# Building part of the expert gates by scatter-add instead of one-hot matmuls, and moving gathered rows between two passes

## The reference

```
q = x @ w_q                                   # 8 heads, two halves of 64
s = q . keys                                  # 2 x 128 scores per head
top_s, top_i = top_k(s, 16)                   # on each half
best_s, best_j = top_k(top_s[0] + top_s[1], 16)
expert = i1 * 128 + i2                        # 8 heads x 16 experts per token
g = softmax(best_s)
act = gelu(u[expert] . x) * g                 # u, v: tables of 16384 x 1024
y = sum over the 128 choices of act * v[expert]
```

## Time and profile before

| | us |
|---|---|
| median of 3 runs (lowest, highest) | 2739.08 (2737.34, 2743.43) |
| the profiled execution, its span | 2744.57, 2742.8 |
| PE busy | 2465.3 (90%) |
| DVE busy | 2131.3 (78%) |
| ACT busy | 1234.8 (45%) |
| POOL busy | 571.3 (21%) |

### The profile page before, as it was taken

One profiled execution on the slowest core, in us unless ns is written; L12 is line 12 of the kernel. 1 busy time (PEld: TensorE's weight loads), 2 busy tenths in 40 slices (PEclk: granted clock), 3 DMA queues, 4 the chain that ended last, 5 costly groups with the idle time before them and its releaser, 6 DMA issues.

```text
span 2742.8 us, 36197 instructions
## 1 busy us (share of the span) xinstructions
PE 2465.3 (90%) x10956; PEld 1938.4 (71%) x10956; DVE 2131.3 (78%) x3891; ACT 1234.8 (45%) x2704; POOL 571.3 (21%) x408
## 2 busy tenths in 40 slices
PE   4987888999899787899999999998878999999996
PEld 3767766666456576777777777776756888878885
DVE  4877613666388855889999999989688888888888
ACT  2332043444312142267777787777433333333333
POOL 2013104422032320011111111112122323232221
PEclk9999999999999899999999999999988999999998
DMA  6646651112032325478888888888899999999996
GB/s 275 217 163 253 255 218 62 62 62 86 23 117 101 146 78 217 136 263 309 322 299 319 298 319 309 305 304 313 318 387 347 381 382 388 384 368 380 389 382 237
DMA packets 223810, 697.60 MB, mean 254 GB/s; under 512 B 15840, under 2 KB 111456, under 8 KB 181472
## 3 DMA queue, kind: packets, MB, share of 16 engines
q1 hardware_dynamic: 165984, 367.25, 37.2%
q0 software_dynamic: 37632, 270.55, 26.0%
q10 hardware_dynamic: 20096, 58.72, 5.6%
HBM read 614.67 MB, written 81.79 MB: 254 GB/s over the span
## 4 chain that ended last, share of the span: by engine, by line
PE 42%; DVE 32%; DVEq 9%; DMA 8%; issue 5%; ACT 3%; SPq 1%; ACTq 1%; POOL 0%; PEldq 0%; PEld 0%
PE ps L866 21%; PE ps L557 7%; DVE g_acc L1787 5%; DVEq L1799 4%; PE ps L542 4%; DVE rows L1778 4%; DVE arena L1454 3%; DMA act_in<-act_scratch 3%; DVE hot L1741 2%; PE ps L569 2%; DMA arena<-in_weights 2%; DVE cand L1397 1%; PE ps L905 1%; DMA rows<-in_rows,pick_e 1%; DMA ring<-in_weights 1%
## 5 line engine op out<-in xcount | busy, mean ns | idle before, releaser
L1999 POOL DMA_INDIRECT rows<-in_rows,pick_e x256 | 333.4, 1302 | 1350.1 <-DVE g_acc L1787 1188.6
L1245 ACT CAST t_hi<-raw 128x1024 fp32r<-128x1024 f32 x256 | 268.8, 1050 | 545.0 <-PE ps L866 528.1
L866 PE MATMUL ps<-t_hi,c_hi 128*128 128x512 f32 x1024 | 407.4, 398 | 37.9 <-DVE t_lo L1859 33.0
L866 PE MATMUL ps<-n_hi,t_hi 128*128 128x512 f32 x1024 | 413.6, 404 | 26.4 <-DVE t_lo L1804 25.3
L866 PE MATMUL ps<-t_lo,c_hi 128*128 128x512 f32 x1024 | 404.4, 395 | 0.0
L866 PE MATMUL ps<-t_hi,c_lo 128*128 128x512 f32 x1024 | 404.1, 395 | 0.0
L866 PE MATMUL ps<-n_hi,t_lo 128*128 128x512 f32 x1024 | 401.2, 392 | 0.0
L866 PE MATMUL ps<-n_lo,t_hi 128*128 128x512 f32 x1024 | 401.0, 392 | 0.0
L1787 DVE SCALAR_TENSOR_TENSOR g_acc<-rows,small,g_acc 128x1024 f32<-128x1024 f32 x254 | 326.3, 1285 | 34.9 <-issue 9.1
L1934 POOL TENSOR_TENSOR w_lo<-ring,w_hi 128x1024 fp32r<-128x1024 f32 x76 | 189.4, 2498 | 667.2 <-ACT w_hi L998 559.9
L866 PEld LDWEIGHTS ps<-t_hi,c_hi 128*128 128x128 f32 x1024 | 196.2, 192 | 85.3 <-issue 44.5
(11 more groups left out here) (198 smaller groups left out, 4188.4 us busy)
## 6 DMA issues: line engine op xcount, KB each, us to landing
raw<-in_table SPq DMA_DIRECT2D x256, 512.0 KB, 7.2
ring<-in_weights SPq DMA_DIRECT2D x44, 2048.0 KB, 8.2
act_scratch<-act_out SPq DMA_DIRECT2D x128, 256.0 KB, 3.5
gate_scratch<-staged ACTq DMA_DIRECT2D x16, 2048.0 KB, 9.7
act_in<-act_scratch SPq DMA_DIRECT2D x128, 256.0 KB, 10.6
gate_in<-gate_scratch SPq DMA_DIRECT2D x32, 1024.0 KB, 15.6
arena<-in_weights ACTq DMA_DIRECT2D x24, 1024.0 KB, 9.4
arena<-in_weights SPq DMA_DIRECT2D x2, 2048.0 KB, 21.2
```

The costliest lines, as they stand in the source:

```text
L866: last = mm(out, a, b_, start=start and x == 0, stop=stop and x == len(pairs) - 1, skip_group_check=True)
L1245: copy(t_hi[:, t % 2, :], raw[:, t % 4, :]).then_inc(hi_ready, 1)
L1999: G.indirect_dma_start(rows[:, j % 4, :], None, rows_in, bass.IndirectOffsetOnAxis(ap=pick_e[:, j:j + 1], axis=0)).then_inc(row_in[j % 4], 16)
```

## The change

The gates of blocks 2 and 3 are made by scatters. Half of `gate_scratch` is filled with zeros while the trunk runs (`clear` on SP, 16 transfers of 1 MB from a zeroed buffer). The searches of blocks 2 and 3 go in pairs, one head of both blocks at a time (`PAIRS`). After a pair DVE works out each choice's place in `gate_scratch` (`place_pair`), ACT takes the exponential (`exp_pair`), DVE normalizes (`weigh_pair`), and POOL issues 32 indirect DMAs (`scatter`), each of which adds one number for each of 128 tokens into memory. All 256 of them stand on the queue of the gathers, two or three a body.

The gates of blocks 0 and 1 are made by one-hots as before, in 64 steps instead of 128: steps 0 to 31 in every second body from 26 to 88, steps 32 to 63 in each of the bodies 90 to 121. In the first 32 ACT makes `hot1` too, in the others DVE makes it. Blocks are turned at bodies 25 and 89.

Bodies 0 to 23 do two search parts each and no slot; bodies 24 to 103 one search part and one slot; bodies 104 to 127 two slots and no search. The v pass takes exactly one slot a tile. `load_gates(0, 0)` stands behind the last store of activations. DVE and ACT run the v pass in straight code, and the last steps of the prompt's first block are done three tiles of four later.

```diff
-STEPS = SEQS[1] // 4
+STEPS = 2 * P // 4
+DENSE = 24
+TURN_AT = (25, 89)
+PAIRS = ((2, 0), (0, 0), (0, 1), (2, 1), (0, 2), (0, 3), (2, 2), (1, 0), (2, 3), (1, 1), (2, 4), (1, 2), (2, 5), (1, 3),
+         (2, 6), (2, 7))
...
         def slots_of(k):
+            if k < DENSE:
                 return ()
+            if k < P - DENSE:
+                return (k - DENSE,)
+            if k < P:
+                j = P - 2 * DENSE + 2 * (k - P + DENSE)
                 return (j, j + 1)
+            return (k,)
...
         def steps_of(k):
+            if k < 26 or k > 121 or (k < 90 and k % 2):
                 return ()
+            return ((k - 26) // 2,) if k < 90 else (k - 58,)
...
+                def clear(c):
+                    sp.dma_start(gate_zero[c + ZEROS], score_in[:, 1].rearrange("p a n -> p (a n)").unsqueeze(1).broadcast_to(
+                        (P, 8, 2 * P))).then_inc(zeroed, 16)
...
             store_act(P - 1)
+            for half in range(2):
+                sp.wait_ge(gates_stored[half], 16 * STEPS // 16)
+                sp.wait_ge(scattered[half], 16 * TOPK * HEADS)
+            load_gates(0, 0)
...
             def scale_hot(s):
...
                 for x in range(4):
+                    if s < 32:
+                        A(hot1[:, s % 2, x, :], iota, ACT.Abs, bias=sel_n[:, 0, col + x:col + x + 1])
+                    A(hot2[:, s % 2, x, :], iota, ACT.Abs, bias=sel_n[:, 1, col + x:col + x + 1])
+                act.drain()
+                if s < 32:
+                    A(hot1[:, s % 2], hot1[:, s % 2], ACT.Relu, bias=ones[:, 0:1], scale=-1.0)
+                for x in range(4):
                     last = A(hot2g[:, s % 2, x, :], hot2[:, s % 2, x, :], ACT.Relu,
...
             for k in range(P):
+                t = k % 4
                 split_tile(k // 4, t + 1)
+                if k and pair_of(k - 1) is not None:
+                    exp_pair(pair_of(k - 1))
+                if k + 1 in TURN_AT:
+                    exp_block(0, 1, 2 + TURN_AT.index(k + 1))
...
+            def place_pair(p):
+                o, n = P + 32 * (p % 2), 32 * p
+                keys1, keys2, v = (sel[:, x, o:o + 32] for x in range(3))
+                stt(out=keys1, in0=keys1, scalar=float(P), in1=keys2, op0=ALU.mult, op1=ALU.add)
+                V.tensor_copy(gsum[:, 0:2], v.rearrange("p (h k) -> p h k", k=TOPK)[:, :, 0])
+                dve.drain()
+                tt(v.rearrange("p (h k) -> p h k", k=TOPK), v.rearrange("p (h k) -> p h k", k=TOPK),
+                   gsum[:, 0:2].unsqueeze(2).broadcast_to((P, 2, TOPK)), ALU.subtract).then_inc(pair_shifted, 1)
+                for x in range(2):
+                    ts(cell[:, n + TOPK * x:n + TOPK * (x + 1)], keys1[:, TOPK * x:TOPK * (x + 1)], float(STAGE),
+                       token[:, x:x + 1], ALU.mult, ALU.add)
...
             for k in range(P):
                 for s in steps_of(k):
-                    hot_keys(s)
+                    if s >= 32:
+                        hot_keys(s)
...
+            def scatter(n):
+                b, h = n // TOPK % 2, n // (2 * TOPK)
+                if n % (2 * TOPK) == 0:
+                    pool.wait_ge(pair_ready, h + 1)
+                if n % TOPK == 0:
+                    after(pool, scattered[b], 16 * TOPK * h)
+                G.indirect_dma_start(gate_cells, bass.IndirectOffsetOnAxis(ap=cell[:, n:n + 1], axis=0),
+                                     cell_g[:, n:n + 1], None, compute_op=ALU.add).then_inc(scattered[b], 16)
...
+                known = 2 * TOPK * sum(pair_of(x) is not None for x in range(min(k, P)))
+                pace = 3 if k < DENSE or k % 2 == 0 else 2
+                while sent < known and (pace > 0 or k == P - 1):
+                    scatter(sent)
```

More of the change, by code:

```diff
@@ L375, in load @@
                     load_unit(weights[UNITS_ADA + n], (b + n) % 2)
+                    if g and n == 2:
+                        sp.wait_ge(zero_ready, 1)
+                        for c in range(4):
+                            clear(c)
                 if g == 0:
@@ L463, in _ @@
                 load_tile(k + 4)
[L464 to L473, removed]
+                for x in range(2, 2 * len(PAIRS)):
+                    if starts(x - 1) == k:
+                        load_scores(sp, False, x)
                 if k == P // 2:
@@ L1346, in root, with turn @@
                 A(var[:, x:x + 1], var[:, x:x + 1], ACT.Sqrt).then_inc(y_rstd, 1)
-            def turn(i, t, static=None, last=False):
+            def turn(i, t, last=False):
                 if not (last and t == 3):
@@ L1818, in _ @@
                     use_slot(j)
+                if k and pair_of(k - 1) is not None:
+                    weigh_pair(pair_of(k - 1))
+                if k + 1 in TURN_AT:
+                    norm_block(0, 1, 2 + TURN_AT.index(k + 1), sel[:, 2, 0:P], sel_ready)
                 m, parts = search_of(k)
+                b, h = at_of(m)
                 for part in parts:
-                    search(False, m, P * (m // 8 % 2) + 16 * (m % 8), part)
-                if block is not None and t == 2:
-                    half = block % 2
-                    norm_block(half, 1, block, sel[:, 2, half * P:(half + 1) * P], sel_ready)
+                    if (b, h, part) == (1, 0, 3):
+                        dve.wait_ge(sel_turned, 1)
+                    search(False, m, P + 16 * (2 * (scattered_before(m) % 2) + b - 2) if b >= 2 else 16 * h, part)
+                if pair_of(k) is not None:
+                    place_pair(pair_of(k))
+                if k + 2 in TURN_AT:
+                    shift_block(0, 1)
             coefficient(0, 0, 0)
@@ L1844, in finish_gathered, with turn @@
                 tt(y, y, f_x1a[:, x, :], ALU.add).then_inc(y_ready, 1)
-            def turn(i, t, half, static=None, last=False):
-                if static is not None:
-                    slots = slots_of(static)
-                    use_slot(slots[0])
-                else:
-                    dve.wait_ge(row_in[t], 16 * i + 16 * (P // 4 + 1))
-                    V.tensor_tensor_reduce(out=rows[:, t, 0:D], in0=rows[:, t, 0:D], in1=x_tok[:, 1, :], scale=1.0,
-                                           scalar=0.0, op0=ALU.mult, op1=ALU.add, accum_out=dot[:, t:t + 1]
-                                           ).then_inc(dotted, 1)
+            def turn(i, t, half, last=False):
+                slots = slots_of(P + 4 * i + t)
+                use_slot(slots[0])
                 if not (last and t == 3):
@@ L1860, in turn @@
                        ALU.subtract).then_inc(lo_ready, 1)
-                if static is not None:
-                    for j in slots[1:]:
-                        use_slot(j)
+                for j in slots[1:]:
+                    use_slot(j)
                 if not (last and t >= 2):
@@ L2025, in shape_constants @@
     c[:, C_IOTA:C_IOTA + P] = np.arange(P)
+    for x in range(2):
+        t = np.arange(P) + (2 + x) * P
+        c[:, C_TOKEN + x] = (t // STAGE) * (P * P * STAGE) + t % STAGE
     for n, w in enumerate(WINDOWS):
```

212 lines of the change are left out of this document (102 added, 110 removed).

## The result

The changed kernel takes 2764.36 us (median of 4 runs, 2762.83 to 2766.73) against 2740.47 beside it: a ratio of 1.0087, interval 1.0075 to 1.0099. It is slower, where 2713 was forecast. The profiled spans are 2762.5 and 2742.8 us, 19.7 apart. The starts of DVE's lower halves (t_lo, one a tile) cut both spans; "mark 27" is the lower half that is made in body 26.

A forecast was written before the change was run, and what follows sets the result against it. DVE bounded the u tiles, TensorE and DMA the v pass, DMA the doubled v tiles. Terms -2 + 1.6 + 3 + 4 + 6 + 3 - 42 = -26.4 from 2739.1 gave 2713 us; own range 2690 to 2731, with rivals 2672 to 2788.

The forecast's parts named there:

- 24 x 8.5 = 204: Bodies 104 to 127: DMA bytes bound, 8.3 us a tile plus scatters, 204 us against 198 before, so +6.
- rival B: Doubled u tiles wait for gather landings: 9.5 us each, 24 us more, 2737 in total, no change; chance 0.15.
- a gather's 1.0: POOL's queue: a scatter's issue taken as 1.0 us like a gather's, between nothing and 1.6.
- 12.2 us forecast: Last u body to first v matmul: the gate load waits for the last Gelu; 12.2 us against 9.2, +3.
- rival A: DVE sets the pace of bodies 26 to 89: 12.4 us a pair, 404 instead of 447, total 2670; chance 0.14.
- 14.5 for five: Bodies 26 to 89: four exp_pair and one exp_block, with table loads, add 2.9 us each to ACT's loop.
- 708 forecast: V pass: 128 tiles at 5.5 us plus 4 for a lower clock, 708 against 749.6 before, -42.
- slot for slot it has what the steady stretch has: V pass: the new one's slots match the old steady stretch, so every tile runs at 5.5 us.
- The trunk's clears: Trunk: 16 clears of 1 MB hide behind weight loads and cost nothing; uncovered, 45 us.
- Bodies 90 to 103: One gate step and one slot as before, 14 x 6.94, plus two pairs' work: +4 us.
- Rival C: Scatter packets load the DMA engines: gain gone at 0.07 us a packet, 2790 at 98 ns; chance 0.21.
- my 16: Scatter packets on the DMA engines: 16 ns each, 20 packets a tile, 0.3 us in 17 doubled tiles.

The follow-up runs named there:

- e10: e8 with gathers of 4 KB in place of 8 KB, so other values; ratio 0.9859 to the kernel before.
- e2: Changed kernel with five row buffers instead of four, gathers issued three slots ahead, c_lo over the searches' buffers; ratio 1.0064 to the kernel before.
- e11: e8 with each 2 MB gate store sent as four pieces in four successive steps; ratio 0.9926 to the kernel before.
- e1: Changed kernel without its 256 scatters and SyncE's wait for them, gates of blocks 2 and 3 left out; ratio 1.0041 to the kernel before.
- e16: Changed kernel with three semaphore-ordered memsets on POOL in place of each scatter, no packets; ratio 1.0087 to the kernel before.
- e3: Changed kernel with the first gate load issued ahead of the last two stores of activations; ratio 1.0075 to the kernel before.
- e9: e8 without the fifth row buffer; ratio 0.9985 to the kernel before.
- e13: e9 with only c_lo moved to the place of the searches' buffers; ratio 1.0033 to the kernel before.
- e8: Changed kernel with five row buffers, early gate load, late add, DVE's first one-hot and later exponential together; 2720.68 us, ratio 0.9945 to the kernel before.
- e4: Changed kernel with the v pass's row_add and its drain moved behind c_lo, t_lo and the coefficients; ratio 1.0039 to the kernel before.
- e15: Changed kernel with memsets on POOL, ordered by drains, in place of scatters; ratio 1.1192 to the kernel before.
- e14: e11 with c_lo back at the end of SBUF and c_hi in the searches' place; ratio 0.9937 to the kernel before.
- e17: e11 with c_hi and c_lo both at SBUF's end, half the gate buffer in the staging tile; 2703.34 us, 0.9874 of the kernel before.

## Why the prediction failed

**Doubled u tiles: the step that failed first.** "24 x 8.5 = 204" took DMA bytes as the bound. e10 halves the gathers' bytes and gains 9 us; e2 keeps every byte and gains 15. What holds is rival B's loop, which I had at 0.15: a gather leaves only after the add of four slots back. It came to 9.4 us a tile, and B's price was 9.5. That these agree is in part luck: the code waits for the add four slots back, not three, and that add stands behind the next slot's dot, so the loop spans three slots, one and a half tiles. A landing of 8.9 us and 2.9 for dot, add and hand-over (1978.08 to 1980.96 in that chain) are 11.8 us, an estimate of 7.9 a tile. Scatters ahead of the gathers, landings of up to 15.3 and gate stores (e11) make the rest. I had set B aside by the doubled v tiles, 8.7 us with the same landing; those had no scatters beside them. A scatter holds POOL's queue for 1.86 us where I took a gather's 1.0, out of a range to 1.6, and this loop has no room for it. e1 (-18.6) and e2 (-15.2) agree, and e16 gives the queue's time half of it or more.

**Into the v pass.** The mechanism was right, the sizes were not: 12.2 us forecast, 21.7 measured. I let the last Gelu fall before mark 128 and the load fly 10.5 us; the Gelu came 2.9 after it, behind a gather that landed late, and the load took 15.3. With four row buffers, moving it up brings the way down to 9.5, 15.3 and 9.6 us (e3, e9, e13), though e3's ratio shows only 3 us of it; with five, the load leaves early but flies 22.5 us (e8).

**Bodies 26 to 89.** The loop was sized right: 6.18 + 7.04 + 6.50 + 7.33 is 27.05 us for four tiles, 13.5 for two, so rival A fell. The failed term is the exponential: 14.5 for five, measured 458.6 - 32 x 13.5 = 26.6. ACT pays the 2.8 us forecast, but tiles 32 to 34 take 24.4 in place of 19.7: 4.7 each, and the turn at 88 to 90 some 6. Of the 1.9 us that a pair costs beyond the 2.8, 0.6 fall in tile 32, ahead of the exponential; where the rest comes from is open. The Trainium skill (ScalarE: Activation LUTs, What ACT_TABLE_LOAD costs) would give 27 by its drain; that is the right sum by another way, since no gap of 1.4 us stands between the load and Exp.

**V pass.** 708 forecast, 722.7 measured. 5.529 for 5.5 us a tile makes 4; it would have been 5.44 with the order of the old loop, which I took to be no matter ("slot for slot it has what the steady stretch has"): the change also put the add ahead of c_lo and t_lo (e4, 13 us). The rest lies in the first 30 tiles, 181.2 us instead of 166, of which I had put down 4 for the clock (its mean from 2018 to 2115 was 0.94): in the chain an `act_in` load of 20.2 us at the eighth tile, which SP issues behind five loads for the last stage. Issuing these takes SP from 2035.06 to 2042.68, the first alone 5.4 us:
```profile
2035.06 5.41 SPq L527 DMA_DIRECT2D staged<-in_g_final  x1
```
How much of the 15 us they cost was not tried.

**What held.** The trunk's clears cost nothing that shows. Bodies 90 to 103 came at +3.6. Rival C's condition was not met: q0's share rose from 26.0% to 28.7%,
```profile
q0 software_dynamic: 74496, 270.70, 28.7%
```
12685 - 11410 = 1275 us for 36864 more packets (144 a scatter, not the 128 of the forecast), 35 ns each on the mean, under C's 70. It was above my 16, though, in a stretch where the DMA share is 0.97: 44 scatters of 144 packets cost 14 us on 16 engines by that figure, of which e16 leaves 10 at most to lengthen the tiles. That a write under 512 B is a read and a write, as the Trainium skill has it (DMA: Bandwidth & Descriptors, Specifications), may be in these 35 ns. The 0.2 to 2 us of a memory access, which the Trainium skill gives in the same page's section Latency and other measured facts, are not.

## What to carry to other kernels

Ask of every added DMA what it holds of its issuer's queue, not only of the wire: here a scatter of 4 bytes a row held GpSimd longer (1.8 us) than a gather of 8 KB a row (1.1 to 1.7), and whatever is queued behind it is late. A stall inside a loop over several engines can cost more than its own length (2.8 us of ACT came with 4.7 here), so don't price it by its engine's rows alone. When a loop is rewritten, compare the order of each engine's instructions with the old one: an add moved ahead of two subtractions cost 13 us here.

## What the runs showed of the hardware

- Indirect scatters of 128 x 4 bytes went out every 1.86 us at best (1.55 and 0.30 between), and lasted 1.78 on the mean. Gathers of 128 x 8 KB lasted 1.1 to 1.2 on the mean in the changed kernel, but 1.6 in the steady v pass of the kernel before and 1.66 in that of e8 (2250 to 2600).
- A drain on POOL behind a gather took 5.4 us on the mean (e15).
- Where an operand of the matmul lies in SBUF sets its pace: with c_lo or c_hi in the place of the searches' buffers, 231 (e13) and 233 ns (e14) a matmul of 512 columns at a granted clock of 1.00 (5.55 and 5.60 us over 24), and 227 with both at the end of SBUF (5.44; e9, e17). Why is open.
